# A three-layer fp32 block on one Trainium2 core: the last layer's attention scores as stacked fp32r passes, and two of four weight scalings on ScalarE

## The chip, the cores and the metric

The kernel runs on one core of one Trainium2 chip. The core has TensorE (PE; its weight loads are PEld in the profile), VectorE (DVE), ScalarE (ACT), GpSimd (POOL, unused here) and SyncE (SP), which issues the loads. The metric is device time in microseconds of one execution; three runs of the kernel before gave 1940.8 to 1941.73, median 1941.08.

## The reference

The block takes x of 256 tokens by 2048 features through three layers: a latent attention, an mLSTM mixer, and a last layer with four mixers side by side and a feed-forward part. All arithmetic is fp32. The change lies in the first of the four mixers, an attention with 8 heads of 64 features in 2 groups (heads 0 to 3 share one key, heads 4 to 7 the other). Cut to it:

```python
q = rms_norm(q, q_gain)                       # 256 x 8 x 64
k_s, k_w = rms_norm(k_s, k_gain), rms_norm(k_w, k_gain)   # 256 x 2 x 64 each
s_s = einsum('btgrd,bgtkld->bgrtkl', q, k_s blocks) * scale + bias   # "selected"
s_w = einsum('btgrd,bsgd->bgrts', q, k_w) * scale + bias             # window
p = masked_softmax(s, mask)                   # each of the two by itself
o = g0 * o_cmp + g1 * (p_s @ v_s) + g2 * (p_w @ v_w)   # g = sigmoid(gates)
```

With 256 tokens both the selected and the window attention see every earlier key, so a head has two score matrices of 256 x 256, causal.

## The kernel before

Every large product is (x high + x low) times (w high + w low) without the low-low term, with the halves in fp32r: ScalarE copies a loaded weight half of 128x1024 to its high part (`hi`, L1635), VectorE subtracts to get the low part (`lo`, L2137), and TensorE reads both through `mm` (L1208). There are four slots of such halves; `hi` of slot s waits until TensorE has closed slot s-4, `lo` waits for `hi`.

The order of all work is written out by a planner (`plan`). It appends steps with `say(what, n)` to one list for each section; each engine's program walks the same list and does its part of each step, in that order. Nothing is reordered later: an engine whose step waits stays there. The weight tiles of the long projections ("tile") are spread between the steps as filler, four tiles a piece.

The stretch of the change is the section "nsa". The filler there is the projection "b" and then "wo2". `p.pipe` (L767) runs the heads through the stages a0 to a7; in each step the stages come in the order 7, 6, 5, 1, 4, 3, 2, 0, with filler ahead of 6, 1, 4 and 0, and each stage is of another head:

- a0 (PE): the scores of head h, in plain fp32, into banks 3 and 4: 512 columns for the later 128 queries (selected and window keys), 256 for the earlier 128. The stationary operand is a 128x128 block of queries, 64 rows of head h and 64 of head h+4; the keys of the other group are zeros (`kswn`). It waits until VectorE has read the banks for the head before (s_n2s).
- a1 (DVE, L2851 to L2856): scale and bias the scores into SBUF (L2851, L2852, which frees the banks), then the negated maxima.
- a2 (ACT, L2067): four exps with a sum each. a3 (DVE, L2860 to L2863): reciprocal, times the gates, then four scalings of the weights, two of 256 columns and two of 128.
- a4 (PE): six transposes (L1587 to L1589), waits for a3. a5 (ACT, L2074, L2075): copies them out. a6 (PE): times the values. a7 (ACT, L2079): copies the result.

One step reads, from the written order, "a3 of head 2, a2 of head 3, gn square 0, four tiles, hi 346, a0 of head 5, a6 of head 0, a5 of head 1, gn fold 0, two tiles, lo 346, two tiles, a1 of head 5". The others between a2 and a0: nothing for a0 of head 3; sg 3, two tiles, lo 344, two tiles for head 4; four tiles, hi 347 for head 6. "gn square" is a 128x1024 square on ScalarE, "gn fold" two adds on VectorE, "gn total" a root on ScalarE (L1644, L1645), "sg" three instructions of VectorE (L2821, L2823), "b out" a copy on ScalarE (L1640) and an add on VectorE (L2154) that waits for it.

Ahead of it, in the section "d", the keys and queries are normalized: "qk scaled" (L2679 for queries, L2683 for keys into zero-padded places, L2687 the zeros), and "sg stats" and "sg norm" (L2799 to L2810) stand right around a0 of head 0.

Of the kernel before, what the change touches and what calls it, by code (L numbers as in the profile page):

```python
# [15 lines left out]
T = 256  # L16
# [402 lines left out]
def plan():  # L419
# [221 lines left out]
    def d_and_cmp():  # L641
        g = p.proj(st["d"])
        for b in range(8):
# [3 lines left out]
            if b in CMP_AT:  # L647
# [11 lines left out]
             29: [("qk scaled", 2)]}  # L659
# [12 lines left out]
    for step in (("nsa gates", 0), ("cmp gelu", 0), ("zeros", 3), ("zeros", 0)):  # L672
        say(*step)
        go(dv, 1)
# [27 lines left out]
    def d5(h):  # L702
        say("d5", h)
        if h == 7:
            say("sg gelu", 0)

# [46 lines left out]
    def a0(h):  # L753
        say("a0", h)

# [11 lines left out]
    p.pipe(8, ["a0", a1, "a2", "a3", "a4", "a5", "a6", a7], wos, 46, (6, 1, 4, 0), (7, 6, 5, 1, 4, 3, 2, 0),  # L767
# [73 lines left out]
def build(nc, dr, out):  # L841
    with ExitStack() as ctx:
# [184 lines left out]
        KZ = ar(5120, 544)  # L1027
        kswn, kcz = [ar(5120, 512), blk(RAW, 6, 2)], ar(5632, 32)
# [37 lines left out]
        def by_token(n, half):  # L1066
# [42 lines left out]
        s_m0, s_m1, s_m2, s_m4, s_m3, s_m5, s_mnum, s_msq, s_mcap, s_mden, s_mrs = (  # L1109
            sem("s_ml_" + n) for n in ("spread", "sc", "dec", "exp", "wt", "pv", "num", "sq", "cap", "den", "rs"))  # L1110
# [14 lines left out]

        s_sgel, s_sgst, s_sgrs, s_sgn, s_sgm, s_sgo = (sem("s_sg_" + n) for n in ("gel", "st", "rs", "nm", "mm", "out"))
# [12 lines left out]
        s_tap, s_conv, s_zsl, s_raws, s_us = (sem("s_" + n) for n in ("tap", "conv", "zsl", "raws", "us"))  # L1139
# [59 lines left out]
        def pe_program():  # L1199
# [340 lines left out]
            for what, h in pl.steps["nsa"] + pl.steps["wo2"]:  # L1540
# [18 lines left out]
                elif what == "gn part":  # L1559
                    b = GN_BANK[3]  # L1560
                    if h == 0:
                        take(b)
                    pe.wait_ge(s_n9, h + 1)
                    ins = mm(bank[b][:, 0:T], ones, blk(CV, h), h == 0, h == 3)
                    if h == 3:
                        ins.then_inc(s_gtot, 1)
                    free[b] = s_grs, 4
                elif what == "a0":
                    X1, Y1 = bank[3], bank[4]
                    take(3)  # L1570
# [47 lines left out]
        def act_program():  # L1618
# [245 lines left out]
            for what, n in pl.steps["mlstm"] + pl.steps["mz"] + pl.steps["wo1"]:  # L1864
# [3 lines left out]
                elif what == "m1":  # L1868
                    D = Dt[h % 2]
                    if h == 0:  # L1870
                        ac.wait_ge(s_gates, 5)
                        ac.activation(den, den, ACT.Exp).then_inc(s_mcap, 1)
# [21 lines left out]
                elif what == "cell sums":  # L1894
                    ac.wait_ge(s_mden, 1)
                    ac.activation(den, den, ACT.Square, scale=(256 * EPS) ** 0.5).then_inc(s_mden, 1)
                    ac.wait_ge(s_mden, 3)
                    rstd(rsh, ssq, 256, 4).then_inc(s_mrs, 1)
# [24 lines left out]
            for what, n in pl.steps["p1"] + pl.steps["d"]:  # L1923
# [37 lines left out]
                elif what == "qk rstd":  # L1961
# [3 lines left out]
                    rstd(rs6, bank[7][:, :], 64, 0).then_inc(s_qrs, 1)  # L1965
                elif what == "cmp gelu":
# [21 lines left out]
            for what, n in pl.steps["stick"]:  # L1988
# [39 lines left out]
            for what, n in pl.steps["nsa"] + pl.steps["wo2"]:  # L2028
# [3 lines left out]
                elif what == "b out":  # L2032
                    b_half(n)
                elif what == "sg gelu":
# [28 lines left out]
                elif what == "a2":  # L2063
# [4 lines left out]
                    ins.then_inc(s_n3, 1)  # L2068
                elif what == "a5":
# [54 lines left out]
        def dve_program():  # L2124
# [388 lines left out]
            for what, n in pl.steps["mlstm"] + pl.steps["mz"] + pl.steps["wo1"]:  # L2513
# [26 lines left out]
                elif what == "cell sums":  # L2540
# [3 lines left out]
                    dv.wait_ge(s_mcap, 1)  # L2544
# [3 lines left out]
                    dv.wait_ge(s_mden, 2)  # L2548
                    dv.wait_ge(s_msq, 16)
                    stt(ssq, den, 1e30, ssq, ALU.min, ALU.add).then_inc(s_mden, 1)  # L2550
                elif what == "mz cell":
                    if h == 0:
                        dv.wait_ge(s_mrs, 1)
                        dv.wait_ge(s_oex, 8)
# [34 lines left out]
            for what, n in pl.steps["p1"] + pl.steps["d"]:  # L2589
# [61 lines left out]
                elif what == "zeros":  # L2651
# [4 lines left out]
                    elif n == 2:  # L2656
                        dv.memset(KZ, 0.0)
# [15 lines left out]
                elif what == "qk scaled":  # L2673
                    dv.wait_ge(s_qrs, n + 1)
                    for j in range(2):
                        m = (0, 2, 6)[n] + j
                        src = blk(RAW, m)
                        if m < 4:
                            ins = stt(blk(QZ, m), src, pcol("q_gain", 0), rs6[:, j * T:(j + 1) * T], ALU.mult, ALU.mult)  # L2679
                        else:  # L2680
# [44 lines left out]
            for what, n in pl.steps["stick"]:  # L2725
# [20 lines left out]
                elif what == "cz weights":  # L2746
# [8 lines left out]
                       czs.rearrange("p (s n) -> p s n", n=1).broadcast_to([128, 16, 15]), ALU.mult).then_inc(s_cz, 1)  # L2755
                elif what == "d2":
# [30 lines left out]
            for what, n in pl.steps["nsa"] + pl.steps["wo2"]:  # L2787
# [3 lines left out]
                elif what == "b out":  # L2791
                    b_out(n)
                elif what == "b conv":
# [63 lines left out]
                elif what == "a3":  # L2857
# [3 lines left out]
                    chain(tt(sm[i], sm[i], GX[:, 6 * h:6 * h + 4], ALU.mult))  # L2861
                    for s, ap in enumerate(seg(h)):
# [197 lines left out]
```

## Time and profile before

| | |
|---|---|
| three runs | 1941.73, 1941.08, 1940.8 us |
| the profiled execution | 1940.91 us, span 1939.4 us |
| busy over the span | PE 100%, PEld 85%, DVE 70%, ACT 52% |
| granted TensorE clock | 1.00 throughout |
| the heads' scores on PE (a0) | 1035.7 to 1081 us of the span |

The span is from the first to the last instruction; the execution's own time is 1.5 us longer. A busy PE is one whose matmuls overlap without a gap; ends of matmuls are modelled. Times in the views are microseconds from the span's start.

### The profile page before, as it was taken

The page shows a single profiled execution, that of the slowest core. Times are in us where ns is not written, and L with a number is a line of the kernel's source. Part 1 is how long each engine was busy: PE and PEld are TensorE (multiplying, and loading weights), DVE is VectorE, ACT ScalarE, POOL GpSimd, SP SyncE. Part 2 cuts the span into 40 slices and gives each one's busy share as a digit, 9 for nine tenths or more (in the row PEclk, how much of TensorE's full clock was granted, in tenths as well). Part 3 has the DMA queues.
Part 4 walks back from the last instruction along what each step waited for, and adds up shares of the span by engine and source line. Part 5 has one row for each costly group of instructions (what it writes and reads, how often), then busy time and mean ns, then how long its engine had stood idle before and what let it go on. Part 6 is the DMA issues. An engine that isn't in the chain of part 4 may idle for free.

```text
span 1939.4 us, 25500 instructions
## 1 busy us (share of the span) xinstructions
PE 1933.9 (100%) x10006; PEld 1647.0 (85%) x10006; DVE 1358.0 (70%) x2011; ACT 1001.2 (52%) x1433; POOL 0.2 (0%) x4
## 2 busy tenths in 40 slices
PE   9999999999999999999999999999999999999999
PEld 7889988988888888898888888888888888888887
DVE  6756778887555687998788887489666444666654
ACT  5645554675556554585566655444444334444442
POOL 0000000000000000000000000000000000000000
DMA  8454325455544455545534345555555555555563
GB/s 327 178 193 175 129 90 193 176 196 185 192 172 152 174 195 196 195 174 198 217 114 157 116 155 196 197 190 185 187 193 205 198 202 192 190 185 195 186 227 108
DMA packets 51706, 353.21 MB, mean 182 GB/s; under 512 B 5652, under 2 KB 7196, under 8 KB 9860
## 3 DMA queue, kind: packets, MB, share of 16 engines
q1 hardware_dynamic: 50016, 348.84, 49.0%
q10 hardware_dynamic: 1572, 2.75, 0.4%
q8 instruction: 79, 1.29, 0.3%
q14 instruction: 39, 0.32, 0.0%
HBM read 349.47 MB, written 2.11 MB: 181 GB/s over the span
## 4 chain that ended last, share of the span: by engine, by line
PE 94%; DVE 4%; ACT 1%; issue 0%; ACTq 0%; DVEq 0%
PE bank L1208 94%; DVE WL L2137 2%; DVE AR L2314 0%; ACT WH L1635 0%; DVE AR L2427 0%; DVE XP L2310 0%; DVE AR L2424 0%; DVE XP L2412 0%; PE bank L1353 0%; DVE AR L2303 0%; DVE AR L2338 0%; DVE AR L2337 0%; ACT XP L1766 0%; ACT L1648 0%; PE bank L1587 0%
## 5 line engine op out<-in xcount | busy, mean ns | idle before, releaser
L1635 ACT ACTIVATE WH<-raw 128x1024 fp32r<-128x1024 f32 x649 | 683.5, 1057 | 655.8 <-PE bank L1208 648.1
L2137 DVE TENSOR_TENSOR WL<-raw,WH 128x1024 fp32r<-128x1024 f32 x649 | 784.8, 1222 | 316.3 <-ACT WH L1635 312.7
L1208 PE MATMUL bank<-XP,WH 128*128 128x512 f32 (+2 forms) x1584 | 498.5, 389 | 0.4 <-DVE XP L2412 0.2
L1208 PE MATMUL bank<-WH,FP 128*128 128x512 f32 x1408 | 434.8, 389 | 0.0
L1208 PEld LDWEIGHTS bank<-XP,WL 128*128 128x128 f32 x1504 | 281.8, 187 | 59.4 <-issue 0.7
L1208 PEld LDWEIGHTS bank<-WH,FP 128*128 128x128 f32 x1408 | 264.3, 188 | 55.7 <-DVE WL L2137 1.0
L1208 PE MATMUL bank<-XP,WL 128*128 128x256 f32 (+1 forms) x1504 | 308.5, 279 | 0.1
L1208 PE MATMUL bank<-WH,XP 128*128 128x512 f32 (+1 forms) x960 | 299.5, 388 | 0.3 <-DVE WL L2137 0.3
L1208 PE MATMUL bank<-WL,FP 128*128 128x512 f32 x704 | 273.9, 389 | 0.0
L1208 PEld LDWEIGHTS bank<-XP,WH 128*128 128x128 f32 (+1 forms) x1584 | 248.0, 187 | 7.4 <-issue 1.4
L1208 PE MATMUL bank<-WH,AP 128*128 128x512 f32 x704 | 217.0, 389 | 0.0
L1208 PEld LDWEIGHTS bank<-WH,XP 128*128 128x128 f32 x960 | 178.7, 188 | 35.0 <-DVE WL L2137 0.5
L1208 PE MATMUL bank<-WL,XP 128*128 128x512 f32 (+1 forms) x480 | 183.7, 383 | 0.0
L1208 PEld LDWEIGHTS bank<-WL,FP 128*128 128x128 f32 x704 | 132.2, 188 | 27.4
L1208 PEld LDWEIGHTS bank<-WH,AP 128*128 128x128 f32 x704 | 132.2, 188 | 27.3
L1208 PE MATMUL bank<-WL,AP 128*128 128x512 f32 x352 | 136.9, 389 | 0.0
L1208 PEld LDWEIGHTS bank<-WL,XP 128*128 128x128 f32 x480 | 90.3, 188 | 16.4
L1208 PE MATMUL bank<-AR 128*128 128x256 f32 (+4 forms) x400 | 90.5, 346 | 0.4 <-DVE AR L2852 0.3
L1208 PEld LDWEIGHTS bank<-AR 128*128 128x128 f32 x400 | 71.8, 189 | 13.9 <-issue 3.8
L1208 PE MATMUL bank<-HP,WH 128*128 128x512 f32 x256 | 81.8, 397 | 0.0
L2907 DVE STREAM_TRANSPOSE ft<-fu 32x256 f32<-32x256 f32 x176 | 76.7, 436 | 2.9
L1208 PEld LDWEIGHTS bank<-WL,AP 128*128 128x128 f32 x352 | 66.1, 188 | 13.8
(339 smaller groups left out, 1632.0 us busy)
## 6 DMA issues: line engine op xcount, KB each, us to landing
raw<-in_W SPq DMA_DIRECT2D x326, 1024.0 KB, 4.8
out<-XT ACTq DMA_DIRECT2D x8, 256.0 KB, 2.1
raw<-in_W SPq DMA_DIRECT2D x3, 512.0 KB, 6.8
X<-in_x SPq DMA_DIRECT2D x3, 512.0 KB, 12.4
AR<-rv SPq DMA_DIRECT2D x1, 1024.0 KB, 5.8
cst<-in_cst SPq DMA_DIRECT2D x1, 899.5 KB, 11.2
raw<-in_W SPq DMA_DIRECT2D x2, 256.0 KB, 4.3
AR<-in_sgu SPq DMA_DIRECT2D x1, 512.0 KB, 5.7
```

What stands on the lines that cost most here:

```text
L1208: return pe.matmul(o, lhsT, rhs, start=start, stop=stop)
L1635: ac.activation(w_slot(WH, s), raw_half(hf), ACT.Copy).then_inc(s_hi, 1)
L2137: tt(w_slot(WL, s), raw_half(pl.half_of[s]), w_slot(WH, s).bitcast(F32), ALU.subtract).then_inc(s_lo, 1)
L2907: ins = dv.transpose(dst[32 * b:32 * b + 32, :, 32 * a:32 * a + 32], src[32 * a:32 * a + 32, :, 32 * b:32 * b + 32])
```

## The change

- Keys. "qk scaled" writes the normalized keys unpadded (`KN`). A new step "k high" (ACT) copies them to fp32r in both halves of the partitions for group 0 (`KH[0]`) and to one half for group 1; a new step "k low" (DVE) subtracts to get the low parts: doubled for group 0 (`KL`), once for group 1 (in the free half of `KH[1]`). After a0 of head 1, "k turn" (ACT) doubles group 1's low and high parts. The large zero fills go.
- Queries. For each head "q high" (ACT, 64x256) and "q low" (DVE, 64x256) make a stationary operand of 128 rows: 64 rows high, 64 rows low, in two buffers. They are said for head h+1 right after a0 of head h, for head 0 in the section "stick".
- Scores. a0 is four fp32r matmuls: stacked queries times doubled high keys, then times doubled low keys, for 512 and for 256 columns. It waits for "q low" of its head, and at head 4 for "k turn".
- Weights. In a3 VectorE makes the four factors and signals (s_nw), and scales only the two narrow parts; ScalarE scales the two wide ones, as a new a3 in its program, and a4 waits for both.
- Three semaphores of the mLSTM layer (s_mcap, s_mden, s_mrs) become one, with the same waits.

```diff
-             29: [("qk scaled", 2)]}
+             29: [("qk scaled", 2)], 30: ["k high"]}
...
     for step in (("nsa gates", 0), ("cmp gelu", 0), ("zeros", 3), ("zeros", 0)):
+        if step[0] == "cmp gelu":
+            say("k low")
...
     def d5(h):
         say("d5", h)
+        if h == 6:
+            say("q high", 0)
         if h == 7:
             say("sg gelu", 0)
+            say("q low", 0)
...
     def a0(h):
         say("a0", h)
+        if h < 7:
+            say("q high", h + 1)
+            say("q low", h + 1)
+        if h == 1:
+            say("k turn")
...
-                    if h == 0:
-                        pe.wait_ge(s_qsc, 4)
-                    q = blk(QZ, h % 4)
-                    k = kswn[h // 4]
-                    mm(X1[:, 0:512], q[:, 128:256], k, True, True)
-                    mm(Y1[:, 0:256].rearrange("p (s k) -> p s k", s=2), q[:, 0:128],
-                       k.rearrange("p (s k) -> p s k", s=2)[:, :, 0:128], True, True).then_inc(s_n1, 1)
+                    if h == 4:
+                        pe.wait_ge(s_kh, 6)
+                    pe.wait_ge(s_kl, 3 + h + 1)
+                    q = QS[h % 2]
+                    two = lambda ap: ap.rearrange("p (s k) -> p s k", s=2)
+                    k, kl = two(KH[h // 4][:, :]), two(KL[:, :]) if h < 4 else KL1
+                    mm(two(X1[:, 0:512]), q[:, 128:256], k, True, False)
+                    mm(two(X1[:, 0:512]), q[:, 128:256], kl, False, True)
+                    mm(two(Y1[:, 0:256]), q[:, 0:128], k[:, :, 0:128], True, False)
+                    mm(two(Y1[:, 0:256]), q[:, 0:128], kl[:, :, 0:128], False, True).then_inc(s_n1, 1)
...
                     pe.wait_ge(s_n4, h + 1)
+                    pe.wait_ge(s_n4a, h + 1)
...
+                elif what == "k high":
+                    ac.wait_ge(s_qsc, 3)
+                    for g, half in ((1, 1), (0, 0), (0, 1)):
+                        ac.activation(KH[g][64 * half:64 * half + 64, :], KN[64 * g:64 * g + 64, :],
+                                      ACT.Copy).then_inc(s_kh, 1)
...
+            def q_high(h):
+
+                sl = slice(64 * (h // 4), 64 * (h // 4) + 64)
+                if h >= 2:
+                    ac.wait_ge(s_n1, h - 1)
+                ac.activation(QS[h % 2][sl, :], blk(QZ, h % 4)[sl, :], ACT.Copy).then_inc(s_qh, 1)
...
+                elif what == "k turn":
+                    ac.wait_ge(s_g7, 8)
+                    two = lambda ap: ap.rearrange("p (s k) -> p s k", s=2)
+                    for half in range(2):
+                        ac.activation(KL1[64 * half:64 * half + 64], two(KH[1][0:64, :].bitcast(F32)),
+                                      ACT.Copy).then_inc(s_kh, 1)
+                    ac.wait_ge(s_kh, 5)
+                    ac.activation(KH[1][0:64, :], KH[1][64:128, :].bitcast(F32), ACT.Copy).then_inc(s_kh, 1)
...
+                elif what == "a3":
+                    i = h % 4
+                    ac.wait_ge(s_nw, h + 1)
+                    for s in (0, 1):
+                        ap = seg(h)[s]
+                        ins = ac.activation(ap, ap, ACT.Copy, scale=sm[i][:, s:s + 1])
+                    ins.then_inc(s_n4a, 1)
...
                     elif n == 2:
-                        dv.memset(KZ, 0.0)
+                        dv.memset(kcz, 0.0)
...
-                            for half in range(2):
-                                sl = slice(64 * half, 64 * half + 64)
-                                ins = stt(blk(kswn[half], j)[sl, :], src[sl, :], pcol("k_gain", 0, sl),
-                                          rs6[sl, j * T:(j + 1) * T], ALU.mult, ALU.mult)
-                    if n == 2:
-                        chain(ins)
-                        ins = dv.memset(RAW[0:64, 6 * T:8 * T], 0.0)
+                        to, gain = (blk(QZ, m), "q_gain") if m < 4 else (blk(KN, j), "k_gain")
+                        ins = stt(to, src, pcol(gain, 0), rs6[:, j * T:(j + 1) * T], ALU.mult, ALU.mult)
                     ins.then_inc(s_qsc, 1)
+                elif what == "k low":
+                    dv.wait_ge(s_kh, 3)
+                    for i, (to, rows, h_) in enumerate(((KH[1][0:64, :], slice(64, 128), KH[1]),
+                                                        (KL[64:128, :], slice(0, 64), KH[0]),
+                                                        (KL[0:64, :], slice(0, 64), KH[0]))):
+                        if i:
+                            dv.wait_ge(s_kl, i)
+                        tt(to, KN[rows, :], h_[rows, :].bitcast(F32), ALU.subtract).then_inc(s_kl, 1)
...
+            def q_low(h):
+
+                sl, to = slice(64 * (h // 4), 64 * (h // 4) + 64), slice(64 - 64 * (h // 4), 128 - 64 * (h // 4))
+                dv.wait_ge(s_qh, h + 1)
+                tt(QS[h % 2][to, :], blk(QZ, h % 4)[sl, :], QS[h % 2][sl, :].bitcast(F32), ALU.subtract).then_inc(s_kl, 1)
...
                     chain(dv.reciprocal(sm[i], sm[i]))
-                    chain(tt(sm[i], sm[i], GX[:, 6 * h:6 * h + 4], ALU.mult))
-                    for s, ap in enumerate(seg(h)):
+                    tt(sm[i], sm[i], GX[:, 6 * h:6 * h + 4], ALU.mult).then_inc(s_nw, 1)
+                    dv.wait_ge(s_nw, h + 1)
+                    for s in (2, 3):
+                        ap = seg(h)[s]
                         ins = ts(ap, ap, sm[i][:, s:s + 1], None, ALU.mult)
                     ins.then_inc(s_n4, 1)
```

## Rows read from the trace of the kernel before

**Rows 1.** The page: busy time, share of the span and instructions; then the chain by engine.
```profile
PE 1933.9 (100%) x10006; PEld 1647.0 (85%) x10006; DVE 1358.0 (70%) x2011; ACT 1001.2 (52%) x1433; POOL 0.2 (0%) x4
...
PE 94%; DVE 4%; ACT 1%; issue 0%; ACTq 0%; DVEq 0%
```
**Rows 2.** Busy time of each engine in 1036:1104 (us, share of slices, clock, DMA).
```profile
1036.00:1104.00 68.00, 67.75 (x375) 57.01 (x374) 62.15 (x142) 44.93 (x123) 0.00 (x0) 1.00 0.34 120
```
**Rows 3.** Timeline of PE (start us, us, engine, line, operation, tiles, count), around head 3's scores.
```profile
1052.14 0.40 PE L1208 MATMUL bank<-XP,WL 128*128 128x256 f32 x2
...
1054.13 0.40 PE L1208 MATMUL bank<-XP,WL 128*128 128x256 f32 x2
...
1054.83 0.40 PE L1208 MATMUL bank<-XP,WL 128*128 128x256 f32 x2
```
**Rows 4.** Timeline of PE, head 7's scores (idle before, releaser), head 4's turn.
```profile
1079.59 1.53 PE L1208 MATMUL bank<-AR 128*128 128x512 f32 x4 [0.25 <-DVE AR L2852]
...
1085.94 0.27 PE L1587 MATMUL bank<-cst,AR 128*128 128x128 f32 x1
```
**Rows 5.** Waits in 1036:1080 (us in total, times, longest).
```profile
PEld bank L1208 <- DVE AR L2852: 0.7, 2, 0.5
```
**Rows 6.** Timeline of ACT in the attention stretch.
```profile
1036.18 1.07 ACT L1635 ACTIVATE WH<-raw 128x1024 fp32r<-128x1024 f32 x1
...
1044.19 0.38 ACT L1640 ACTIVATE AR<-bank 128x256 f32<-128x256 f32 x1 [3.94 <-PE bank L1208]
...
1048.87 0.49 ACT L2067 ACTIVATE AR<-AR,small 128x256 f32<-128x256 f32 x1
...
1062.79 0.50 ACT L2067 ACTIVATE AR<-AR,small 128x256 f32<-128x256 f32 x1
...
1064.55 1.05 ACT L2050 ACTIVATE AR<-AR 128x1024 f32<-128x1024 f32 x1
1065.49 1.05 ACT L1635 ACTIVATE WH<-raw 128x1024 fp32r<-128x1024 f32 x1
```
**Rows 7.** Timeline of DVE in the attention stretch.
```profile
1035.95 1.23 DVE L2806 TENSOR_TENSOR AR<-AR,cst 128x1024 f32<-128x1024 f32 x1 [0.90 <-DMA mu_acc<-in_sgu]
...
1041.71 0.41 DVE L2856 TENSOR_REDUCE small<-AR 128x2 f32<-128x256 f32 x1
...
1054.51 0.16 DVE L2861 TENSOR_TENSOR small<-small,AR 128x4 f32<-128x4 f32 x1
...
1055.62 1.22 DVE L2137 TENSOR_TENSOR WL<-raw,WH 128x1024 fp32r<-128x1024 f32 x1
...
1067.25 0.16 DVE L2861 TENSOR_TENSOR small<-small,AR 128x4 f32<-128x4 f32 x1
...
1068.37 0.68 DVE L2826 TENSOR_TENSOR AR<-AR 128x512 f32<-128x512 f32 x1
...
1072.75 0.16 DVE L2861 TENSOR_TENSOR small<-small,AR 128x4 f32<-128x4 f32 x1
...
1073.87 1.22 DVE L2137 TENSOR_TENSOR WL<-raw,WH 128x1024 fp32r<-128x1024 f32 x1
1078.09 0.42 DVE L2154 TENSOR_TENSOR AR<-bank,AR 128x256 f32<-128x256 f32 x1 [3.00 <-ACT AR L1640]
...
1079.03 0.42 DVE L2852 SCALAR_TENSOR_TENSOR AR<-bank,AR 128x256 f32<-128x256 f32 x1
```
**Rows 8.** Instructions by line and form, ACT, whole span (busy us, mean ns, idle before).
```profile
L2079 ACT ACTIVATE AR<-bank 64x256 f32<-64x256 f32 x8 | 3.0, 377 | 1.8 <-PE bank L1208 1.7
...
L1645 ACT ACTIVATE AR<-AR 128x512 f32<-128x512 f32 x3 | 1.9, 632 | 0.1
```
**Rows 9.** The same of DVE: the nearest forms to the new ones.
```profile
L2563 DVE TENSOR_TENSOR AR<-AR 128x512 f32<-128x512 f32 x8 | 5.5, 692 | 8.4 <-ACT AR L1907 8.4
...
L2839 DVE TENSOR_TENSOR GN<-AR,GN 128x256 fp32r<-128x256 f32 x8 | 3.4, 419 | 0.0
```
**Rows 10.** Timeline of DVE where the keys are prepared.
```profile
948.38 1.17 DVE L2692 COPY cst<-bank 15x128 f32<-15x128 f32 x4 [3.51 <-PE bank L1208]
```

More of the change, by code:

```diff
@@ L766, in plan @@
     wos = fill()
-    p.pipe(8, ["a0", a1, "a2", "a3", "a4", "a5", "a6", a7], wos, 46, (6, 1, 4, 0), (7, 6, 5, 1, 4, 3, 2, 0),
+    p.pipe(8, [a0, a1, "a2", "a3", "a4", "a5", "a6", a7], wos, 46, (6, 1, 4, 0), (7, 6, 5, 1, 4, 3, 2, 0),
            [4] * 6 + [3] * 2 + [5] * 4 + [6] * 3)
@@ L1025, in build @@
         zb = ar(WK + 2048, 960).rearrange("p (l i g n) -> p l i g n", l=16, i=2, g=2)
-        KZ = ar(5120, 544)
-        kswn, kcz = [ar(5120, 512), blk(RAW, 6, 2)], ar(5632, 32)
+        kcz = ar(WK + 5976, 32)
+        KN, KL = blk(RAW, 6, 2), ar_r("KL", 7680, 512)
+        KH = [ar_r(f"KH{g}", 5120 + 512 * g, 512) for g in range(2)]
+        KX = ar_r("KX", WK + 768, 1280)
+        KL1 = bass.AP(KX[:, :].tensor, KX[:, :].offset, [list(KX[:, :].ap[0]), [1024, 2], [1, 256]])
+        QS = [ar_r(f"QS{i}", 13824 + 256 * i, 256) for i in range(2)]
         kcn_, sqk_ = kcn[:, 0:15], sqk[:, 0:15]
@@ L1106, in build @@
         s_e3, s_qk, s_gates = sem("s_e3"), sem("s_qk"), sem("s_gates")
-        s_m0, s_m1, s_m2, s_m4, s_m3, s_m5, s_mnum, s_msq, s_mcap, s_mden, s_mrs = (
-            sem("s_ml_" + n) for n in ("spread", "sc", "dec", "exp", "wt", "pv", "num", "sq", "cap", "den", "rs"))
+        s_m0, s_m1, s_m2, s_m4, s_m3, s_m5, s_mnum, s_msq, s_mden = (
+            sem("s_ml_" + n) for n in ("spread", "sc", "dec", "exp", "wt", "pv", "num", "sq", "den"))
         s_oln, s_oex, s_oh, s_zg, s_ztr, s_zbl, s_zhi, s_zlo = (
@@ L1124, in build @@
         s_cz = sem("s_cz")
+        s_nw, s_n4a = sem("s_at_wt"), sem("s_at_nma")
+        s_kh, s_kl, s_qh = (sem("s_" + n) for n in ("kh", "kl", "qh"))
         s_sgel, s_sgst, s_sgrs, s_sgn, s_sgm, s_sgo = (sem("s_sg_" + n) for n in ("gel", "st", "rs", "nm", "mm", "out"))
@@ L1137, in build @@
         s_dnf = sem("s_dnf")
-        s_tap, s_conv, s_zsl, s_raws, s_us = (sem("s_" + n) for n in ("tap", "conv", "zsl", "raws", "us"))
+        s_tap, s_conv, s_raws, s_us = (sem("s_" + n) for n in ("tap", "conv", "raws", "us"))
         def outed(name, n, half=0):
@@ L1871, in act_program @@
                         ac.wait_ge(s_gates, 5)
-                        ac.activation(den, den, ACT.Exp).then_inc(s_mcap, 1)
+                        ac.activation(den, den, ACT.Exp).then_inc(s_mden, 1)
                     ac.wait_ge(s_m2, h + 1)
@@ L1894, in act_program @@
                 elif what == "cell sums":
-                    ac.wait_ge(s_mden, 1)
+                    ac.wait_ge(s_mden, 2)
                     ac.activation(den, den, ACT.Square, scale=(256 * EPS) ** 0.5).then_inc(s_mden, 1)
-                    ac.wait_ge(s_mden, 3)
-                    rstd(rsh, ssq, 256, 4).then_inc(s_mrs, 1)
+                    ac.wait_ge(s_mden, 4)
+                    rstd(rsh, ssq, 256, 4).then_inc(s_mden, 1)
                 elif what == "o end":
@@ L2022, in act_program @@
                     ac.activation(lA[h % 4], zA[h % 4], ACT.Exp).then_inc(s_g5e, 1)
+                elif what == "q high":
+                    q_high(n)
                 elif what == "sg gelu":
@@ L2033, in act_program @@
                     b_half(n)
+                elif what == "q high":
+                    q_high(n)
+                elif what == "k turn":
[6 more added lines that the diff above has]
+                    ac.activation(KH[1][0:64, :], KH[1][64:128, :].bitcast(F32), ACT.Copy).then_inc(s_kh, 1)
                 elif what == "sg gelu":
@@ L2543, in dve_program @@
                     dn = HN.rearrange("p (s v) -> p s v", v=VW)[:, :, T]
-                    dv.wait_ge(s_mcap, 1)
+                    dv.wait_ge(s_mden, 1)
                     dv.wait_ge(s_mnum, 8)
@@ L2547, in dve_program @@
                     stt(den, dn, -1.0, den, ALU.mult, ALU.max).then_inc(s_mden, 1)
-                    dv.wait_ge(s_mden, 2)
+                    dv.wait_ge(s_mden, 3)
                     dv.wait_ge(s_msq, 16)
@@ L2552, in dve_program @@
                     if h == 0:
-                        dv.wait_ge(s_mrs, 1)
+                        dv.wait_ge(s_mden, 5)
                         dv.wait_ge(s_oex, 8)
@@ L2677, in dve_program @@
                         src = blk(RAW, m)
-                        if m < 4:
-                            ins = stt(blk(QZ, m), src, pcol("q_gain", 0), rs6[:, j * T:(j + 1) * T], ALU.mult, ALU.mult)
-                        else:
-                            for half in range(2):
-                                sl = slice(64 * half, 64 * half + 64)
-                                ins = stt(blk(kswn[half], j)[sl, :], src[sl, :], pcol("k_gain", 0, sl),
-                                          rs6[sl, j * T:(j + 1) * T], ALU.mult, ALU.mult)
-                    if n == 2:
-                        chain(ins)
-                        ins = dv.memset(RAW[0:64, 6 * T:8 * T], 0.0)
-                    ins.then_inc(s_qsc, 1)
+                        to, gain = (blk(QZ, m), "q_gain") if m < 4 else (blk(KN, j), "k_gain")
+                        ins = stt(to, src, pcol(gain, 0), rs6[:, j * T:(j + 1) * T], ALU.mult, ALU.mult)
+                    ins.then_inc(s_qsc, 1)
+                elif what == "k low":
[6 more added lines that the diff above has]
+                        tt(to, KN[rows, :], h_[rows, :].bitcast(F32), ALU.subtract).then_inc(s_kl, 1)
                 elif what == "cmp out":
@@ L2755, in dve_program @@
                        czs.rearrange("p (s n) -> p s n", n=1).broadcast_to([128, 16, 15]), ALU.mult).then_inc(s_cz, 1)
+                elif what == "q low":
+                    q_low(n)
                 elif what == "d2":
@@ L2792, in dve_program @@
                     b_out(n)
+                elif what == "q low":
+                    q_low(n)
                 elif what == "b conv":
```

## The prediction

> **What bounds the kernel now.** I read the page first: TensorE is busy in the whole span and the chain that ended last is TensorE for 94% [rows 1]. So a cycle taken from TensorE counts, if it meets no wait. Then the stretch of the change, about 1036 to 1104 us of the span, engine by engine: of 68 us VectorE is busy 62.15, ScalarE 44.93 [rows 2]. VectorE is nearly a second bound there. The waits say the same: TensorE's weight load waits 0.7 us for L2852, VectorE's read of the scores [rows 5], and the matrix part of head 7's scores starts after 0.25 us of idle for the same line [rows 4]. The scores of head h+1 need the two banks that VectorE empties at L2851/L2852 for head h, so whatever makes VectorE late before that line makes TensorE late. Last the timelines of VectorE and ScalarE against the written order: VectorE works without a gap from 1035.95 to about 1075 and has 3.00 us of idle before 1078.09 [rows 7].
>
> **What is taken from TensorE.** Head 3's scores stand between two equal marks of the weight tiles, 1052.14 and 1054.13: 1.99 us, of which two tiles take 0.70 (1054.13 to 1054.83), so a head's scores take 1.29 [rows 3]. Afterwards they are four fp32r matmuls with 512, 512, 256 and 256 columns, the very columns and loads of two tiles: 0.70. Gain 0.59 a head, 8 x 0.59 = 4.7 us. The bounds: not under 0.64 (half of 1.29, if only columns count), not over 1.29 (stacked operands no faster).
>
> **What is added, each at its size.** Keys: VectorE loses two of four scalings, a memset and the chain to it, and gets three 64x512 subtractions, under 0.69 each by the 128x512 form [rows 9], 2.1 us, at about 939.7; five microseconds on it sits idle 3.51 us before 948.38 [rows 10], so I take 0. If that cover failed at the next weight halves, it would cost up to 2.1. The three 64x512 copies on ScalarE ("k high"), under 0.63 each [rows 8], 1.9 us, lie in waits of ScalarE; three more ("k turn") after head 1's scores, before a wait of 3.94 us that ends at 1044.19 [rows 6]: 0, at most 1.9 each if ScalarE had been the late one. Query halves: on ScalarE 64x256, 0.38 as L2079 [rows 8]; on VectorE 64x256 subtracted, under the 0.42 of L2839 [rows 9], and since starts follow each other faster than durations I take 0.35 (0.25 to 0.42). The weights: VectorE's four scalings take 1054.70 to 1055.62, 0.92; without the two wide ones I take 0.39 (bounds 0.2 and 0.92), a saving of 0.53. ScalarE's two wide copies with a scale per partition: the nearest row is the wide exp with a bias per partition, 0.50, of which four (two wide, two narrow, with reads) pass in 1.76, 1062.79 to 1064.55 [rows 6]. I take 0.80 for two (0.6 to 1.2).
> By busy time that would be harmless: VectorE's 0.35 against 0.53 saved, ScalarE some 12 us more on 45 of 68. What decides is the order.
>
> **The wait that is new.** "q low" on VectorE waits for "q high" on ScalarE of the same head, said right before it. In ScalarE's order "q high" of head h+1 stands behind "a3" and "a2" of the same step, and "a3" now waits for VectorE's weights (s_nw). Before, ScalarE ran ahead: its exp "a2" of head 1 began at 1048.87 [rows 6], while VectorE's weights of head 0, said just before, began their last step at 1054.51 [rows 7]. That lead is gone: ScalarE can only start copies, four exps and whatever else is said when VectorE has the weights, and VectorE then stands at "q low" till all of it is done. Behind "q low" queue the next weight low halves, the bias and maxima of the next head (L2851 to L2856), for which TensorE waits.
> Both engines run strictly in their order. The trace has it: the maxima of head 0 were done at 1042.12 (1041.71 + 0.41) [rows 7], but its exp began only behind the L1640 of 1044.19 [rows 6]. By the Trainium skill (TensorE: Matmul & The Clock Gate, Architectural detail: the array is 16x 32x32) ScalarE and VectorE are strict first-in-first-out queues. By that rule the stalls below stand; an engine that could look past the wait would leave the gain of 4.7 whole. The trace agrees with the rule.
>
> **The sum**, as lateness of VectorE against the trace of before.
> 1. "q low" 1 stands before "sg norm", which started at 1035.95. ScalarE's high half there starts at 1036.18 and the next can start 0.95 later, as 1064.55 to 1065.49 [rows 6], at 1037.15; then q high 0.38 to 1037.53, a handover of about 0.1, q low 0.35: 1037.95. Late 2.0.
> 2. "q low" 2 and 3, no stall: 0.7, together 2.7.
> 3. Head 0's weights ended at 1054.67 (1054.51 + 0.16) [rows 7], now + 2.7 = 1057.37. ScalarE: copies 0.80, exps 1.76, q high 0.38, handovers 0.1 = 3.04, to 1060.4. q low 4 to 1060.75, where the trace had 1055.62 [rows 7]. Late 5.1.
> 4. Head 1's weights: "sg" 3 and a weight half lie between and cover the 3.04; the narrow saving goes against q low. Late 5.0.
> 5. Head 2's weights end at 1067.41 + 5.0 = 1072.4. Now "gn square" 0 (0.94) and a high half (0.95) [rows 6] are said before q high as well: 3.04 + 1.89 = 4.93, to 1077.35, q low to 1077.7; the trace had 1068.37 [rows 7]. Late 9.3.
> 6. Head 3's weights end at 1072.91 + 9.3 = 1082.2; with one high half 3.04 + 0.95 = 3.99, to 1086.2, q low 7 to 1086.55 against 1073.87 [rows 7]. Late 12.7.
> 7. Here the trace had the 3.00 us of idle, waiting for ScalarE's half of "b out" 5. ScalarE is the late one now: after 1086.1 it has "a7" 0.3, "a5" 0.75, "gn total" 0.8, "gn square" 0.94, the half 0.38, to 1089.3; against 1078.09 late 11.2. VectorE's read of head 6's scores ended at 1079.45 (1079.03 + 0.42) [rows 7] and ends at 1090.65.
> TensorE's scores of head 7, at 1079.59 before [rows 4], start 11.2 later. It had come with its savings well before, so none of the savings of heads 0 to 6 is left; only head 7's own 0.59 lies behind the last stall. Net 11.2 - 0.6 = +10.6 us. After it there is no "q low" any more. Head 4's turn came at 1085.94 [rows 4], 6.5 us after the read of head 6's scores at 1079.45; between the two VectorE has only the maxima and head 4's weights, under 3 us, so some 3 cover ScalarE's copies. TensorE is the bound again to the end, and gives nothing back.
> The profiled execution took 1940.91 us (span 1939.4 and 1.5 around it), the median is 1941.08, 0.2 more. 1941.0 + 10.6 = 1951.6.
> The bounds of this case: the prices above vary the three stalls of ScalarE's chain (3.0, 4.9, 4.0) by some 15% either way, 1.8; q low by 0.5 in sum; the keys up to +2.1: 1948 to 1956.
>
> **Rivals.**
> A, the gain arrives (faster). For: TensorE hardly waits today, ScalarE is idle a third of the stretch [rows 2], each query half is made one head ahead. If VectorE came to "q low" after ScalarE had been there each time, 1941.0 - 4.7 = 1936.3. Against: VectorE hands ScalarE the start signal itself, and needs 0.39 to reach "q low" where ScalarE needs 3.0. Chance 0.15.
> B, gain and stall cancel. If the stalls of steps 5 and 6 fell into time in which TensorE does not need VectorE (its halves a head ahead, its banks free), only steps 1 to 4 stay: 5.0 late, less 4 x 0.59 gained later = 2.6; 1943.6, and with cheaper copies down to 1939. Against it: the banks' margin is nothing [rows 4, 5]. Chance 0.15.
> C, dearer: a weight half comes late too. In step 4 low half 344 is done at about 1068.2 and TensorE wants it near 1069.2; 1 us more on ScalarE's chain turns it into another wait each step, and the keys' 2.1 show: 1957 and more. Chance 0.05.
> D, the stacked pass is no faster on TensorE (the change doesn't do what it says). Since TensorE waits at each of those scores anyway this costs only head 7's 0.6: 1952.2, inside the forecast.
>
> **Chances.** The forecast with D 0.65, A 0.15, B 0.15, C 0.05. Within 0.2% is 1937.2 to 1945.0 (below that a measurement here tells nothing): B, rounded 0.15. Faster 0.15 from A, slower 0.70 from forecast and C. The range leaves out A and C: 1938 to 1956; the forecast's own is 1948 to 1956.
>
> **What would show it.** VectorE's idle time before the 64x256 subtraction in "q low", released by ScalarE: about 2.6 (0.9 of it idle before as well), 2.6, 0, 4.5 and 3.6 us for heads 1, 4, 5, 6 and 7, some 13 us in all. TensorE idle before the scores of heads 1, 4, 6 and 7, released by L2852. A head's scores 0.70 on TensorE. ScalarE waiting for VectorE before the first wide copy, over 5 us at head 0. After 1100 us every engine as before, all rows shifted equally. I am wrong if "q low" shows idle of under 1 us each, or if TensorE doesn't wait at the scores although VectorE is late.

## The result, and the profile after

| | before | after |
|---|---|---|
| median of 4 runs, us | 1941.32 | 1962.89 |
| lowest to highest | 1940.80 to 1941.73 | 1962.83 to 1963.34 |
| span of the profiled execution | 1939.4 | 1961.4 |

The change makes the kernel slower: 1.0112 times the time before, 95% interval 1.0100 to 1.0124, or +21.6 us. The forecast was +10.6, with 1956 as the end of its range.

The page of the changed kernel, beside [rows 1]:

```profile
span 1961.4 us, 25532 instructions
PE 1936.9 (99%) x10006; PEld 1649.9 (84%) x10006; DVE 1357.7 (69%) x2003; ACT 1014.7 (52%) x1463; POOL 0.2 (0%) x4
PEclk9999999999999999999999899999999999999999
PE 89%; DVE 7%; ACT 3%; issue 1%; ACTq 0%; DVEq 0%
```

TensorE has as many instructions as before, yet the chain that ended last now runs for 10% through VectorE and ScalarE, and one slice of the granted clock, that of the attention, is lower. A "busy" PE hides the lower clock: its busy time grew by 3.0 us although the scores became cheaper.

The waits of the changed kernel in 1033:1130 (waiting engine and line, what it waited for, us in total, times, longest):

```profile
ACT AR L2119 <- DVE small L2923: 22.1, 7, 7.3
DVE QS L2761 <- ACT QS L2014: 13.3, 5, 4.5
...
PE bank L1225 <- ACT AR L2131: 8.6, 4, 4.8
DVE AR L2206 <- ACT AR L1661: 8.4, 4, 5.1
...
PE bank L1225 <- DVE AR L2914: 5.5, 5, 2.7
...
PE bank L1608 <- ACT AR L2126: 3.6, 2, 2.3
```

ScalarE waits for VectorE's factors (the new a3), VectorE for ScalarE's "q high", and TensorE for both. The line to notice is the third. L2131 is a7, ScalarE's 64x256 copy of a finished head out of bank 7. Before the change TensorE had no wait for it in this stretch; its only waits there were short ones for the scores' banks [rows 4, 5]. The last line is of the same kind: TensorE's transposes wait for a5 (L2126), which stands behind the new a3 too.

VectorE's timeline around "q low" (start, us, engine, line, operation; in brackets the idle time before it and who ended it):

```profile
1037.75 0.42 DVE L2761 TENSOR_TENSOR QS<-AR,QS 64x256 fp32r<-64x256 f32 x1 [2.27 <-ACT QS L2014]
...
1061.01 0.42 DVE L2761 TENSOR_TENSOR QS<-AR,QS 64x256 fp32r<-64x256 f32 x1 [2.65 <-ACT QS L2014]
...
1069.15 0.42 DVE L2761 TENSOR_TENSOR QS<-AR,QS 64x256 fp32r<-64x256 f32 x1 [0.28 <-ACT QS L2014]
...
1078.48 0.42 DVE L2761 TENSOR_TENSOR QS<-AR,QS 64x256 fp32r<-64x256 f32 x1 [4.54 <-ACT QS L2014]
...
1087.59 0.42 DVE L2761 TENSOR_TENSOR QS<-AR,QS 64x256 fp32r<-64x256 f32 x1 [3.59 <-ACT QS L2014]
1094.37 0.42 DVE L2206 TENSOR_TENSOR AR<-bank,AR 128x256 f32<-128x256 f32 x1 [5.10 <-ACT AR L1661]
```

Forecast of these five idle times: 2.6, 2.6, 0, 4.5, 3.6. The large ones came out to the tenth, the first was 0.3 less and the third 0.3 more. The last line is the one that the forecast had not: VectorE waits 5.10 us for its input of "b out" 5, after the last "q low".

ScalarE's timeline says why:

```profile
1083.52 0.91 ACT L2119 ACTIVATE AR<-AR,small 128x256 f32<-128x256 f32 x2 [4.17 <-DVE small L2923]
1084.33 0.49 ACT L2112 ACTIVATE AR<-AR,small 128x256 f32<-128x256 f32 x1
...
1086.09 1.04 ACT L1656 ACTIVATE WH<-raw 128x1024 fp32r<-128x1024 f32 x1
1087.15 0.41 ACT L2014 ACTIVATE QS<-AR 64x256 fp32r<-64x256 f32 x1
1087.58 0.38 ACT L2131 ACTIVATE AR<-bank 64x256 f32<-64x256 f32 x1
...
1092.19 0.47 ACT L1665 ACTIVATE AR<-bank,cst 128x256 f32<-128x256 f32 x1 [3.48 <-PE bank L1225]
```

a7 (1087.58) stands behind the wide scalings, the exps, a weight half and "q high". It empties bank 7, which TensorE's next a6 needs. TensorE, same stretch and after:

```profile
1082.26 0.47 PE L1225 MATMUL bank<-KH,QS 128*128 128x512 f32 x1 [0.57 <-DVE AR L2914]
...
1088.01 1.65 PE L1225 MATMUL bank<-AR 128*128 128x256 f32 x4 [4.82 <-ACT AR L2131]
...
1091.80 0.58 PE L1225 MATMUL bank<-XP,WH 128*128 128x512 f32 x1
...
1095.82 0.47 PE L1225 MATMUL bank<-KH,QS 128*128 128x512 f32 x1 [0.20 <-DVE AR L2914]
...
1101.01 0.96 PE L1225 MATMUL bank<-AR 128*128 128x256 f32 x4 [2.83 <-ACT AR L2131]
...
1110.32 0.92 PE L1225 MATMUL bank<-AR 128*128 128x256 f32 x4 [0.34 <-ACT AR L2131]
...
1112.09 0.47 PE L1225 MATMUL bank<-XP,WH 128*128 128x512 f32 x1
```

TensorE stands 4.82 us at one a6 and 2.83 at the next; head 7's scores, at 1079.59 before [rows 4], start at 1095.82. And after both stops it is slow for a while. Stretches of the changed kernel (busy us and count for PE, weight load, DVE, ACT, POOL; then the granted clock, DMA):

```profile
1084.00:1088.00 4.00, 0.00 (x0) 0.00 (x0) 0.41 (x2) 3.95 (x14) 0.00 (x0) 0.59 0.35 147
1088.00:1092.00 4.00, 3.99 (x13) 3.40 (x14) 1.24 (x2) 0.71 (x2) 0.00 (x0) 0.56 0.00 0
1092.00:1096.00 4.00, 3.79 (x24) 3.16 (x23) 1.60 (x4) 2.11 (x4) 0.00 (x0) 1.00 0.00 0
1101.00:1105.00 4.00, 3.99 (x13) 3.40 (x14) 3.90 (x10) 0.70 (x2) 0.00 (x0) 0.59 0.51 150
...
1036.00:1104.00 68.00, 49.74 (x255) 41.42 (x254) 46.50 (x97) 37.90 (x100) 0.00 (x0) 0.91 0.23 79
1036.00:1126.00 90.00, 70.77 (x375) 59.50 (x374) 61.78 (x133) 56.67 (x151) 0.00 (x0) 0.92 0.26 93
```

A mean of 0.56 is mostly the lower of the two levels (1.2 GHz). The a6 from 1088.01 to 1091.80 takes 3.79 us. The same matmuls in the kernel before, at the full level, take 1.99:

```profile
1082.36 0.81 PE L1208 MATMUL bank<-AR 128*128 128x256 f32 x4
...
1084.35 0.58 PE L1208 MATMUL bank<-XP,WH 128*128 128x512 f32 x1
```

In 1036:1126 TensorE is idle 19.2 us (90 - 70.77): 8.6 for a7, 5.5 for VectorE's reads of the scores, 3.6 for a5 and 1.5 for VectorE's "sg norm". The whole loss is in this stretch: at 930 us, ahead of all new instructions, the rows are already 0.42 us later than before (a difference in the start-up), the keys add nothing, and after 1122 TensorE has no wait that the kernel before did not have.

### The profile page after: what moved, and what is told of

Its sections match the earlier page's. It is cut to its first block, busy times and chain, and to the rows that moved or that the text cites. A ratio compares the mean times of both kernels' runs of the same rounds, so it can differ in the third digit from the quotient of the medians.

```text
span 1961.4 us, 25532 instructions
## 1 busy us (share of the span) xinstructions
PE 1936.9 (99%) x10006; PEld 1649.9 (84%) x10006; DVE 1357.7 (69%) x2003; ACT 1014.7 (52%) x1463; POOL 0.2 (0%) x4
## 4 chain that ended last, share of the span: by engine, by line
PE 89%; DVE 7%; ACT 3%; issue 1%; ACTq 0%; DVEq 0%
PE bank L1225 89%; DVE WL L2189 2%; ACT WH L1656 1%; ACT AR L2112 1%; DVE AR L2366 0%; DVE ft L2971 0%; DVE AR L2479 0%; DVE XP L2362 0%; DVE AR L2476 0%; DVE small L2917 0%; DVE XP L2464 0%; DVE AR L2913 0%; PE bank L1370 0%; ACT AR L2119 0%; DVE AR L2355 0%
## 5 line engine op out<-in xcount | busy, mean ns | idle before, releaser
L1656 ACT ACTIVATE WH<-raw 128x1024 fp32r<-128x1024 f32 x649 | 683.6, 1057 | 652.0 <-PE bank L1225 643.3
L1225 PE MATMUL bank<-AR 128*128 128x256 f32 (+3 forms) x368 | 81.6, 342 | 10.3 <-ACT AR L2131 8.6
L1225 PEld LDWEIGHTS bank<-AR 128*128 128x128 f32 x368 | 67.2, 194 | 21.1 <-ACT AR L2131 9.8
L1225 PEld LDWEIGHTS bank<-WL,AP 128*128 128x128 f32 x352 | 66.1, 188 | 13.8
```

Of the source, the lines that this page charges most:

```text
L1225: return pe.matmul(o, lhsT, rhs, start=start, stop=stop)
L1656: ac.activation(w_slot(WH, s), raw_half(hf), ACT.Copy).then_inc(s_hi, 1)
```

## The experiments

Times are medians beside the kernel before on the same chip (1941.14, 1941.24 and 1941.35 us in the three sets); the ratio has its 95% interval. Theory O is the forecast's ledger (a stall at "q low" chains through VectorE), theory C that the lateness reaches TensorE through other waits, with a lower clock after them.

### Which half of the change costs

**e1_scores_only.** Scores, keys and query halves as changed; VectorE scales all four parts of the weights.

```diff
-                    pe.wait_ge(s_n4a, h + 1)
...
-                    tt(sm[i], sm[i], GX[:, 6 * h:6 * h + 4], ALU.mult).then_inc(s_nw, 1)
-                    dv.wait_ge(s_nw, h + 1)
-                    for s in (2, 3):
-                        ap = seg(h)[s]
+                    chain(tt(sm[i], sm[i], GX[:, 6 * h:6 * h + 4], ALU.mult))
+                    for s, ap in enumerate(seg(h)):
```

> The changed kernel with VectorE scaling all four parts of the weights again; stacked scores, q high and q low stay where they are. Theory O (order): ScalarE waits for nothing of a3, runs ahead again, so q low stalls only at head 1 (2.3 us) and TensorE never waits for a7; VectorE carries 0.35 us more a head until its 3 us of idle, TensorE saves 4.7: 1938 to 1943 us. Rival L (load: the added work itself makes it late, wherever it stands): 1945 or more, with idle before q low as in the changed kernel. Rival W (only the ScalarE scaling costs, q low is harmless): 1936 to 1938.

1944.39 us, +3.3, ratio 1.0016 (1.0007 to 1.0025), 1.4 us above what I expected and 0.6 below the rival L. Only one "q low" still waits (2.3 us); TensorE waits 4.6 us in six waits for VectorE's reads. So here the faster scores do not pay for their two new instructions a head: VectorE is nearly as scarce as TensorE.

**e2_weights_only.** The kernel before, and only the split of the weights' scaling; plain scores. (The three semaphores of the mLSTM layer are one here too.)

```diff
+                elif what == "a3":
+                    ac.wait_ge(s_nw, h + 1)
+                    for s in (0, 1):
+                        ap = seg(h)[s]
+                        ins = ac.activation(ap, ap, ACT.Copy, scale=sm[i][:, s:s + 1])
+                    ins.then_inc(s_n4a, 1)
```

> The kernel before with only the weights split: ScalarE scales the two wide parts, the scores stay plain fp32, no q high or q low. Theory O: ScalarE still waits for VectorE in each a3 (some 20 us in sum), but VectorE has no wait on ScalarE right behind it and saves 0.5 us a head; a7 comes late behind a3, a2 and a weight half, so TensorE waits at the second head's values for about 2 us, and again once: 1942 to 1948 us. Rival W: most of the 21.6 us is here, 1955 or more. Rival L: ScalarE has the room, 1940 to 1942.

1953.12 us, +12.0, ratio 1.0061 (1.0046 to 1.0076). Missed by 5 us, and this was the clue: there is no "q low" in this kernel, and still it loses 12. Its waits in 1033:1130:

```profile
ACT AR L2076 <- DVE small L2870: 18.0, 7, 5.7
...
PE bank L1209 <- ACT AR L2088: 6.1, 3, 3.2
```

L2088 is a7 again. Half of the change, the one that looked harmless by busy time, is the costlier one.

### Take "q low" out of the way

**e3_q_early.** As changed, but the query halves are said two heads ahead, after a1.

```diff
     def a0(h):
         say("a0", h)
-        if h < 7:
-            say("q high", h + 1)
-            say("q low", h + 1)
...
+        if h < 6:
+            say("q high", h + 2)
+            say("q low", h + 2)
```

> The changed kernel with q high and q low of head h+2 said behind a1 of head h, ahead of a3 and a2 (heads 0 and 1 in the section before): no work is removed. Theory O: the idle before q low (13.3 us in the changed kernel) goes to under 1.5, TensorE's waits for L2914 with it; the wait of TensorE for a7 stays in part, since a3 still holds ScalarE: 1943 to 1951 us. Rival L: all the same work is there, so 1958 or more. Rival W: 1958 or more.

1957.86 us, +16.7, ratio 1.0086 (1.0070 to 1.0103). Missed by 6.9 us. The 13.3 us of "q low" stalls are gone from the waits, and only 4.9 us of time with them. By theory O alone most of the loss should have gone. TensorE waits 8.4 us for a7 here (longest 4.4), as in the changed kernel.

**e4_q_early_dve.** The edits of e3 and e1 together.

```diff
+            say("q high", h + 2)
+            say("q low", h + 2)
...
+                    for s, ap in enumerate(seg(h)):
```

> e3 and e1 together: q two heads ahead, VectorE scales all four parts. Theory O: no stall of VectorE before q low at all, ScalarE ahead, TensorE keeps its 4.7 us except what VectorE's 0.35 us a head cost: 1936 to 1940 us, the fastest of these four. Rival L: not under 1943.

1943.18 us, +2.0, ratio 1.0010 (1.0001 to 1.0020). Missed: I expected the gain of 4.7 us once no wait was in the way. In 1036:1104 VectorE is busy 64.12 of 68 us, more than before [rows 2], and TensorE waits 3.9 us for its reads. The rival L, that the added work counts wherever it stands, had "not under 1943" and fits. That what remains is VectorE's work is tested in e11.

### Move the wait

**e5_a3_late.** As changed, but ScalarE takes its two wide scalings last in each step, after everything else, a7 of another head included.

```diff
-(7, 6, 5, 1, 4, 3, 2, 0),
+(7, 6, 5, 1, 4, 3, 2, 0, (3, "a3w")),
...
-                elif what == "a3":
+                elif what == "a3w":
```

> The changed kernel with one thing moved: ScalarE's two wide scalings (and with them its wait for VectorE's weights) are said at the end of the step, behind a2, the weight half and q high. Same work. Theory P (place of the one wait in ScalarE's order): ScalarE reaches a2, q high and a7 without waiting for VectorE, so neither q low nor a7 is late; only head 1's 2.3 us and VectorE's work stay: 1938 to 1944 us. Rival S (the split itself: ScalarE's 0.9 us a head and the second semaphore on a4 make the turns late): 1950 or more.

1945.82 us, +4.6, ratio 1.0023 (1.0014 to 1.0033), a little outside what I expected. One wait moved in one engine's order, not one instruction more or less, and 17.0 of 21.6 us are gone. ScalarE's wait for the factors falls from 22.1 us to 7.3, and TensorE's longest at a7 to 1.55.

**e6_q_early_a3_late.** The edits of e3 and e5 together.

```diff
+            say("q high", h + 2)
...
+(7, 6, 5, 1, 4, 3, 2, 0, (3, "a3w")),
```

> e3 and e5 together: q two heads ahead and the wide scalings at the end of the step. Theory P: the least waiting of all with the whole change in: VectorE has 0.53 us a head less than in e4 and TensorE its 4.7 us, so 1936 to 1940 us, faster than the kernel before. Rival S: 1946 or more.

1945.47 us, +4.2, ratio 1.0022 (1.0013 to 1.0032). Missed, by 5.5 us. TensorE still waits 2.6 us for a7, and VectorE 4.3 us for ScalarE's half of "b out" 5, where it waited 3.00 before the change [rows 7].

### The wait that the ledger left out

**e7_weights_a7_early.** e2, with a7 of a head said in the step of its own a6, before a3 and a2.

```diff
-    p.pipe(8, ["a0", a1, "a2", "a3", "a4", "a5", "a6", a7], wos, 46, (6, 1, 4, 0), (7, 6, 5, 1, 4, 3, 2, 0),
+    p.pipe(8, ["a0", a1, "a2", "a3", "a4", "a5", "a6", lambda h: None], wos, 46, (6, 1, 4, 0),
+           (7, 6, 5, 1, 4, (6, a7), 3, 2, 0),
```

> e2 (plain scores, weights split) with a7 said in the step of its own a6, ahead of a3 and a2, instead of one step later. Theory P: TensorE's wait for a7 (6.1 us in e2) and the slow clock behind it go; the small waits for a5 and the late halves stay: 1943 to 1948 against 1953.1. Rival: if the wait just moves (ScalarE now waits for TensorE's a6 ahead of a3), 1951 or more.

1945.39 us, +4.2, ratio 1.0021 (1.0011 to 1.0030), as expected: 7.7 of e2's 12.0 us were a7's position.

**e13_a7_early.** The changed kernel with this same edit and nothing else.

```diff
-(7, 6, 5, 1, 4, 3, 2, 0),
+(7, 6, 5, 1, 4, (6, a7), 3, 2, 0),
```

> The changed kernel with a7 (the copy that frees bank 7) said in the step of its own a6, ahead of a3 and a2, instead of one step later; q high, q low and both scalings stay where they are. Theory P with the prediction's ledger: what the ledger left out is TensorE's wait for a7 (4.8, 2.8 and 0.3 us in the changed kernel) and the slow clock behind it (some 3.5 us). Without them the ledger's +10.6 should come out: 1950 to 1954 us. Rival: if the ledger was too small in its own terms (q low, scalings), 1957 or more.

1953.33 us, +12.0, ratio 1.0062 (1.0048 to 1.0076). With the forgotten wait removed the kernel takes what the ledger said (+10.6) within 1.4 us. Its waits in 1033:1130:

```profile
ACT AR L2122 <- DVE small L2926: 21.8, 8, 7.3
DVE QS L2764 <- ACT QS L2017: 13.3, 5, 4.5
...
PE bank L1228 <- DVE AR L2917: 6.0, 4, 2.7
```

The "q low" stalls are the same 13.3 us, and no wait of TensorE for a7 is among them. Head 7's scores on its TensorE timeline:

```profile
1091.76 0.47 PE L1228 MATMUL bank<-KH,QS 128*128 128x512 f32 x1 [1.31 <-DVE AR L2917]
```

That is 12.2 us after 1079.59 [rows 4], less than 0.1 of it the start-up in this execution; the ledger had 11.2. TensorE still waits 4.3 us for a5, and its granted clock is still low twice (a mean of 0.95 over 1036:1104, which was 0.91). Both lie ahead of head 7's scores, at which it still stood 1.31 us for VectorE, so they cost no time of their own there.

**e9_late_copies.** The price of one such wait by itself: the kernel before, where head 0's a7 copy is repeated 18 times in a chain, so that bank 7 comes free late once.

```diff
+                    for _ in range(18 if h == 0 else 0):
+                        chain(ac.activation(MIX[sl, (12 + h % 4) * T:(13 + h % 4) * T], bank[7][sl, 0:256], ACT.Copy))
```

> The kernel before, with head 0's a7 copy done 18 times more on ScalarE, chained, some 0.4 us each, about 7.5 us: nothing else is late on purpose. TensorE should then wait once, about 4 to 5 us, at head 1's values. Theory C (an idle TensorE is granted half its clock on return): the granted clock of the 4 us after it is near 0.6 and the time is 1.5 to 2 us more than the idle: 1946 to 1948.5. Rival: the slow stretch in the changed kernel has another cause; clock 1.00, and the time is the idle alone, 1945 to 1946.

1947.05 us, +5.8, ratio 1.0030 (1.0019 to 1.0041). On TensorE's timeline and in its stretches:

```profile
1078.02 1.65 PE L1208 MATMUL bank<-AR 128*128 128x256 f32 x4 [3.96 <-ACT AR L2081]
...
1082.10 0.99 PE L1208 MATMUL bank<-XP,WH 128*128 128x512 f32 x1
```

```profile
1076.00:1080.00 4.00, 1.98 (x6) 1.71 (x7) 0.00 (x0) 2.60 (x7) 0.00 (x0) 0.57 0.00 0
1080.00:1084.00 4.00, 4.00 (x15) 3.37 (x14) 0.00 (x0) 1.27 (x3) 0.00 (x0) 0.57 0.00 0
```

As expected. The execution of the trace took 1947.66 us, 6.4 more than the median before, and idled 3.96 us at the stop. The rest lies in the work after it, which runs at the lower clock: the a6 takes 4.08 us (1078.02 to 1082.10), not 1.99. By the median the whole loss is 1.5 times the stop, by this execution 1.6 times.

### What is left of the idea

**e10_all_early.** The changed kernel with the three moves of order: query halves two heads ahead (e3), a7 early (e13), the wide scalings last (e5).

```diff
+            say("q high", h + 2)
...
+           (7, 6, 5, 1, 4, (6, a7), 3, 2, 0, (3, "a3w")),
```

> The whole change with all three waits put where they are covered: q two heads ahead, a7 in the step of its a6, the wide scalings at the end of the step. Theory P: TensorE waits only for VectorE's read of the scores (as in e6, 2.4 us): 1938 to 1942 us. Rival S: 1945 or more, as e6.

1941.51 us, +0.2, ratio 1.0001 (0.9992 to 1.0010), as expected. The same instructions as in the changed kernel, in another order: 21.4 us less.

**e11_pool_q.** e4 (VectorE scales all weights, halves early) with "q low" on GpSimd, which has nothing else to do.

```diff
+            for h in range(8):
...
+                nc.gpsimd.wait_ge(s_qh, h + 1)
+                nc.gpsimd.tensor_tensor(QS[h % 2][to, :], blk(QZ, h % 4)[sl, :], QS[h % 2][sl, :].bitcast(F32),
+                                        ALU.subtract).then_inc(s_kl, 1)
```

> e4 (q two heads ahead, VectorE scales all four parts) with q low on GpSimd, which has nothing else to do. Theory P: VectorE carries exactly the work of the kernel before, so its 3.9 us of waits at the scores shrink by what eight q low took from it (some 2.5 us): 1938 to 1941.5. Rival: GpSimd takes over 3 us for one, or slows VectorE by sharing its SBUF port: 1943 or more.

1941.18 us, -0.2, ratio 0.9999 (0.9990 to 1.0008), as expected. That is 2.0 us less than e4, so what held e4 back was in good part the work of "q low" on VectorE.

**e12_pool_q_all_early.** e10 and the GpSimd edit of e11: all orders mended and VectorE relieved of both.

```diff
+           (7, 6, 5, 1, 4, (6, a7), 3, 2, 0, (3, "a3w")),
...
+                nc.gpsimd.wait_ge(s_qh, h + 1)
```

> e10 with q low on GpSimd: VectorE is 0.5 us a head lighter than before, ScalarE's waits are all behind cover. Theory P: 1936 to 1940, the fastest. Rival: as in e11, 1942 or more.

1938.92 us, -2.4, ratio 0.9988 (0.9979 to 0.9997): the one version that beats both kernels, by little, but its interval leaves out 1. Its stretch of the attention, beside [rows 2], and the new group on GpSimd:

```profile
1036.00:1104.00 68.00, 66.04 (x382) 57.15 (x382) 59.99 (x129) 57.12 (x151) 6.08 (x6) 1.00 0.34 125
```

```profile
L2853 POOL TENSOR_TENSOR QS<-AR,QS 64x256 fp32r<-64x256 f32 x8 | 7.5, 943 | 1063.3 <-ACT QS L2019 1063.3
```

VectorE is down to 59.99 from 62.15, and TensorE is still idle 2.0 us of 68. That, against 0.25 before, is most of what is missing of the 4.7 us that the scores free.

## Why the prediction was wrong

**What held.** The direction and its mechanism. The stalls at "q low" came out at 2.27, 2.65, 0.28, 4.54 and 3.59 us, 13.3 in all. TensorE's scores were late (less 0.42 of start-up) by 1.8, 4.7 and 9.6 us at heads 1, 4 and 6, where steps 1, 3 and 5 had 2.0, 5.1 and 9.3. ScalarE waited 7.27 us at head 0 ("over 5"). Two scaled copies took 0.81 us to the next start (0.80 taken), and a head's scores in a running TensorE 0.70 (0.70 taken; 1049.28 to the tile at 1049.98). The keys cost nothing. So rival A (the gain arrives) was wrong, and B (gain and stall cancel) too, since the lateness of steps 5 and 6 went through whole. C had the size, "1957 and more", but not the place: no weight half was late on TensorE. D was wrong, the scores are faster, by the 0.59 a head of the forecast. The rule of the Trainium skill (TensorE: Matmul & The Clock Gate, Architectural detail: the array is 16x 32x32) that ScalarE and VectorE are strict first-in-first-out queues held for both engines. Here e5 and e13, which change only ScalarE's order, show what hangs on it: 17.0 and 9.6 us.

**The step that failed is step 7**, and with it the sentence behind it, that TensorE "gives nothing back" once "there is no 'q low' any more". Step 7 walked ScalarE's queue from "q high" on ("after 1086.1 it has 'a7' 0.3, 'a5' 0.75, 'gn total' 0.8, ...") as if all of it could run on. It asked of each entry how long it takes, not who waits for it and what it waits for:

- a7, first in that list, frees bank 7 for TensorE's next a6. TensorE had been there since 1083.19 and stood till 1088.01, 4.82 us.
- Its lower clock then stretched that a6 from 1.99 us to 3.79 (1088.01 to 1091.80).
- "gn total" on ScalarE reads what TensorE makes after this, so ScalarE waited 3.48 us in its turn (1092.19), and VectorE 5.10 before "b out" 5, to 1094.37, where the step had 1089.3.

Head 7's scores came 15.8 us late (16.23 less 0.42), not 11.2. Of these 4.6 us, 3.5 are ScalarE's wait; 1.1 had gathered before in the prices of steps 1 to 6, which put VectorE 12.7 late behind the last "q low", where it was 13.8 (1088.05 against 1073.87, less 0.42). And what lies after them was wrong for the same reason. ScalarE's a3 goes on waiting for VectorE after the last "q low", so a7 stays late: 2.83 us more at 1101.01, again with the lower clock (that a6 took 3.39 us, to the tile at 1104.40, not 1.99), and 0.34 at 1110.32. Head 4's turn of 1085.94 [rows 4] is at 1106.37, or 20.0 later less the start-up, where the ledger had 10.6. These 9.4, the two short waits behind it (0.34 and 0.63, the rest of the 8.6 in the waits) and the 0.4 of start-up make 10.8 of the 11.0 us between forecast and result.

**Shown by runs:** e13 takes a7 out of the queue's back and the time falls by 9.6 us to nearly the forecast's; e7 does the same without any "q low" and gives 7.7; e9 makes one such stop in the old kernel, with its clock. e5 shows the root: with the wait of the new a3 last in ScalarE's step, 17.0 of 21.6 us go, the stalls at "q low" fall from 13.3 to 2.3 and TensorE's waits for a7 from 8.6 to 2.1. **Open:** the parts don't add up simply. Scores alone +3.3, weights alone +12.0, together +21.6: the 6.3 us more fit the order of ScalarE's step (wait, exps, half, "q high", a7), which is long only when both are in; no run separates that sum further.

**The bounds** of the forecast's own case varied prices and "q low" alone. The prices were off by 1.1 us in sum, inside the 1.8 allowed; the range had no place for a wait that isn't in the ledger. The second weakness is that the gain was written as there for the taking: e4 and e6 missed by the same thought. VectorE at 62 of 68 us is a bound beside TensorE, and its new work is paid for in time: with the eight "q low" (3.4 us of its busy time) on GpSimd the kernel was 2.0 and 2.6 us faster (e11 beside e4, e12 beside e10).

## What to carry to other kernels

When an edit makes an in-order engine wait, list all that is queued behind the wait, and for each entry who waits for it: a small copy that frees a PSUM bank can be dearer than the result for which the edit was made. Put a new wait last in its engine's step before judging the edit; here that alone was worth 17 of 21.6 us. And add to a stop of TensorE the slow work that can follow it: here, where the clock fell, the a6 behind a stop of 1.55 to 4.82 us took 1.4 to 2.1 us more than at the full level.

## What the runs showed of the hardware

- The granted clock. In the changed kernel it is at the lower level (0.50 in single microseconds) from about 1084.7, in the midst of the idle time since 1083.19, to about 1091.5, after 3.5 us of work; the stop from 1098.18 to 1101.01 was over before it fell (about 1101.8), and it rose near 1105.2. In e9 it was low from 1076.6 to 1083.4 around a stop that ended at 1078.02. So the fall can come inside the idle time or after it, and what it costs varies: an a6 of 1.99 us took 4.08 in e9, 3.79 and 3.39 here. The stop of 2.71 us before head 4's scores had it too: the mean of 1063:1066 is 0.70 and of 1066:1069 0.73, in time that TensorE lost to VectorE anyway. The length of a stop alone does not tell whether the clock falls. In e4 and e10, with a longest stop of 1.80 and 1.82 us, the mean of 1036:1104 is 1.00; in e6 the clock fell just after the same stop of 1.82 us (it resumed at 1053.83, and 1055:1057 is at 0.50), and in e5 after one of 1.55 us (resumed at 1077.04, 1078:1081 at 0.50), where the a6 took 3.34 us. In e2 a stop of 3.21 us (resumed at 1080.37) had no fall at all. What decides it no run here shows.
- GpSimd took 0.94 us for the 64x256 subtraction that VectorE does in 0.42, 2.2 times as long. The Trainium skill (GPSIMD Engine Reference, Elementwise — side-by-side cycle accounting) has about two times for an addition of two tensors; the trace agrees. On an idle engine the slower instruction was the cheaper one all the same: e11 is 2.0 us faster than e4 and e12 2.6 us faster than e10.
- ScalarE's copy with a scale per partition of 128x256 takes 0.91 us for two that overlap, 0.50 each, as the wide exp, and not the plain copy's 0.38 [rows 6].
